# One 512-column matmul for the high and low inputs of the residual projections, and two broadcasts issued later

## The chip, the cores and the metric

The kernel runs on one core of one Trainium2 chip. The metric is the device time of one execution in microseconds (us), taken as the median of several. TensorE's engines are called PE (matmuls) and PEld (weight loads), VectorE DVE, ScalarE ACT, GpSimd POOL, and SyncE SP.

## The reference

A two-layer block of attention mixers, an indexer, layer norms, a neighbourhood attention, a Fourier mixer, a convolution mixer, cross attention to a memory and convolutional feed-forward nets, on 256 tokens of width 1024, all in float32. What this study is about are the products that are added to the residual stream. There are eight of them, and the first two feed a layer norm:

```
x = layer_norm(ALPHA * x + y @ w_out, ...)     # twice: phases oa, ob
h = h + concat([yf, ya]) @ w_out               # oab
h = h + (gate_b * conv) @ w_out                # oc
h = h + attention(rms(h), memory) @ wo         # ox0, ox1
h = h + (gelu(g) * u) @ w_down                 # fd0, fd1
```

Everything is kept near float32 accuracy by splitting each operand of a projection into a high part (rounded to the matmul's input format) and a low part (what is left), and by adding three products: high x high, high x low, low x high.

## The kernel before

The activations stand as channels x tokens: `h` is the residual stream (128 partitions, 8 tiles of channels, 256 tokens), `xh` and `xl` are the high and low part of the normalised stream, `yh` and `yl` those of a mixer's output.

The weights come from memory in 153 chunks of 1 MB, through four slots `raw` that SP refills. A chunk covers 256 output channels and 1024 input channels, in two halves (`j` = 0, 1) of 128 output channels. For each half ACT writes the high part of the weights, `hi` (L904, `wh`), and DVE the low part, `lo` (L1354, `wl`). PE counts the halves that it has used in `w_used`, and `hi(h)` waits until half h-4 has been used, since `wh` and `wl` hold two chunks.

`project` (L402 and on) multiplies a chunk: for each half 8 tiles `k` of 128 input channels, and for each of these 16 weight tiles three matmuls of 128x128 weights by 256 tokens (L428). A phase is a run of chunks with one operand; its name is that of its weights. With `ready` a phase starts on an operand that is still being made: its first chunk (its first two, where an output takes two chunks) is in the "early" order, which does the tiles 0 to 5 of both halves first, waits for each tile's high part before the first two products and for its low part before the third, and then does tiles 6 and 7. Phases without hooks run their four chunks as two rounds of a loop over the same code, so the early order comes back at every other chunk. `project_tokens` (L499) is for phases whose outputs stand as tokens x channels; its matmuls have 512 columns.

`hooks` are small pieces of work put between the matmuls of a phase, keyed by chunk, half and tile. A norm needs two of them on PE. `stats` (L542) adds the squares (for a layer norm first the values) over the channels; it waits for the sums `acc` that POOL makes (L1846). Then DVE scales them (L1439), POOL takes the power -1/2 (L1863), DVE puts it on a diagonal (L1434), and `bcast` (L549) spreads it over the partitions into bank 5, from where ACT copies it (L988).

In a residual phase each engine does the following for each output (256 channels, one chunk; two chunks in fd0 and fd1, "deep"):

- DVE (`residual`): `x_low` of the output before (L1427), two `lo`, then it waits for PE, and adds the output in PSUM to `h` (L1458; L1461 in oa and ob, where `h` is scaled by ALPHA as well).
- ACT (`residual`): one `hi`, the square of the output before for POOL's sum (L950), one more `hi`, then it waits for DVE's addition and writes `xh` of it (`x_high`, L958). In oa and ob ACT has only the `hi`.
- POOL: it sums the four squares into `acc` (L1846).

The outputs lie in PSUM banks 0 to 3: a phase has a pair (0 and 1, or 2 and 3), an output takes one bank (its two halves side by side), and consecutive phases alternate between the pairs. `enter` waits until the phase before the last, which had the same pair, has been read.

Of the kernel before, what the change touches and what calls it, by code (L numbers as in the profile page):

```python
# [19 lines left out]
F32 = mybir.dt.float32  # L20
# [4 lines left out]
P = 128  # L25
# [49 lines left out]
def schedule():  # L75
# [3 lines left out]
    def add(name, chunks, reader, outs=None, deep=1, wide=False):  # L79
# [7 lines left out]
        p.wide = wide  # L87
# [12 lines left out]
    add("oa", 4, "dve")  # L100
# [6 lines left out]
    add("ob", 4, "dve")  # L107
# [7 lines left out]
    add("oab", 4, "dve")  # L115
    for l in "01":
# [5 lines left out]
        if l == "1":  # L122
            add("oc", 4, "dve")
        add("qx" + l, 4, "dve")
        add("attX" + l, 0, "dve", 4)
        add("ox" + l, 4, "dve")
        add("fu" + l, 8, "dve")
        add("fg" + l, 8, "dve")
        add("fd" + l, 8, "dve", deep=2)
# [46 lines left out]
def build(nc, w, xt, memt, vecs, cst, wkw, dft, rpb, out):  # L176
    ctx = ExitStack()
    with ctx:
# [11 lines left out]
        xh = sb("xh", [P, KT, S], F32R)  # L190
        xl = sb("xl", [P, KT, S], F32R)
        yh = sb("yh", [P, 2 * KT, S], F32R)
        yl = sb("yl", [P, 2 * KT, S], F32R)
# [21 lines left out]
        bank = [ctx.enter_context(nc.psum_tensor(f"bank{i}", [P, 512], F32)) for i in range(8)]  # L215
# [180 lines left out]
        def _(pe):  # L396
            def enter(p):

                if p.before is not None:
                    pe.wait_ge(evac[p.before.reader], p.before.end)  # L400

            def project(name, oh, ol, ready=None, hooks={}, tile0=0):  # L402
# [4 lines left out]
                p = PH[name]  # L407
                enter(p)
                per = 2 * p.deep

                def round_(i, first, hooks=hooks):
                    for c in range(per):
                        n = per * i + (p.n0 + c)
                        slot = (p.n0 + c) % 2
                        b = b3(p.pair + c // p.deep)
                        k0 = (c % p.deep) * KT
# [5 lines left out]
                        def product(k, q, j):  # L422
# [12 lines left out]
                        def steps(j, tiles):  # L435
# [269 lines left out]
            def then(*calls):  # L705
                def f():
                    for call, *args in calls:
# [16 lines left out]
            project("ga", xh, xl, hooks={(1, 0, 2): then((turn_unit, 8)), (1, 1, 3): then((turn_unit, 9)),  # L724
                                         (2, 1, 3): lambda: stats("mem"), (3, 1, 4): lambda: bcast("mem")})
# [129 lines left out]
            for l in "01":  # L855
# [8 lines left out]
                if l == "1":  # L864
                    project("oc", yh, yl, y_ready("conv", g_lo, GBASE["conv"], 2))
# [1196 lines left out]
```

## Time and profile before

| | |
|---|---|
| median of 3 runs | 1037.66 us (1037.25 to 1040.43) |
| the profiled execution | 1037.87 us, span 1036.1 us |
| busy: PE, PEld | 1011.9 us (98%), 945.6 us (91%) |
| busy: DVE, ACT, POOL | 664.6 us (64%), 530.3 us (51%), 165.8 us (16%) |
| mean granted TensorE clock | 0.995 of full speed |
| DMA | 172.56 MB, mean 167 GB/s |

The span is the time from the first to the last instruction of the profiled execution. A busy share is that of the whole span; matmuls overlap their successors in the rows, so the time from one start to the next is what a matmul takes from PE, and its own duration is longer. "Idle" in a row is the time in which the engine stood still just before the instruction, and the name behind it is what it waited for.

### The profile page before, as it was taken

The numbers are of one execution on the slowest core, as the hardware profiler recorded it, in microseconds if no ns is written. First come the engines' busy times: TensorE is split into PE (matmuls) and PEld (weight loads), VectorE is DVE, ScalarE is ACT, GpSimd is POOL, SyncE is SP. The second block draws the span as 40 slices with busy tenths as digits, with TensorE's granted clock in tenths as the row PEclk, the third lists the DMA queues.
The fourth block names the chain that finished last, engine by engine and source line by source line (L and its number), as shares of the span: only waits on it lengthen the run. The fifth ranks groups of instructions, "written<-read, shape, count | busy, mean of one in ns | idle before, by whom it ended". The sixth has DMA issues, their size and how long they took to land.

```text
span 1036.1 us, 18469 instructions
## 1 busy us (share of the span) xinstructions
PE 1011.9 (98%) x7450; PEld 945.6 (91%) x7450; DVE 664.6 (64%) x1022; ACT 530.3 (51%) x804; POOL 165.8 (16%) x146
## 2 busy tenths in 40 slices
PE   9999899999999999999999999999999999999996
PEld 7779669999978998888999999999998999999996
DVE  4779675754457678566456569755576655658852
ACT  4547473454477455455345447544354545436641
POOL 0001022300026231001002005210034200103500
PEclk9999999999999999999999999999999999999998
DMA  9634415465440536425514554447546433455431
GB/s 357 228 122 163 160 45 203 163 221 185 168 157 2 200 141 228 179 88 204 197 45 162 200 203 162 163 176 270 203 163 237 151 141 122 166 200 175 150 122 40
DMA packets 24971, 172.56 MB, mean 167 GB/s; under 512 B 2768, under 2 KB 2896, under 8 KB 4432
## 3 DMA queue, kind: packets, MB, share of 16 engines
q1 hardware_dynamic: 23328, 160.86, 43.4%
q10 hardware_dynamic: 1584, 10.88, 2.7%
q8 instruction: 40, 0.66, 0.2%
q14 instruction: 19, 0.16, 0.0%
HBM read 166.49 MB, written 5.24 MB: 166 GB/s over the span
## 4 chain that ended last, share of the span: by engine, by line
PE 79%; DVE 9%; ACT 5%; issue 3%; DMA 1%; POOL 1%; SPq 1%; POOLq 0%; DVEq 0%; ACTq 0%
PE bank L428 54%; PE bank L499 14%; DVE wl L1354 3%; ACT wh L904 2%; DVE work L1731 2%; PE bank L624 2%; PE bank L578 1%; DMA raw<-w 1%; PE bank L606 1%; POOL acc L1846 1%; DVE work L1734 1%; PE bank L626 1%; PE bank L542 1%; ACT work L1271 1%; PE bank L701 1%
## 5 line engine op out<-in xcount | busy, mean ns | idle before, releaser
L1354 DVE TENSOR_TENSOR wl<-raw,wh 128x1024 fp32r<-128x1024 f32 x300 | 385.1, 1291 | 241.0 <-ACT wh L904 239.9
L904 ACT ACTIVATE wh<-raw 128x1024 fp32r<-128x1024 f32 x300 | 311.9, 1054 | 284.9 <-PE bank L428 221.9
L428 PE MATMUL bank<-xh,wh 128*128 128x256 f32 x1152 | 320.1, 285 | 0.0
L428 PE MATMUL bank<-xh,wl 128*128 128x256 f32 x1152 | 318.0, 283 | 0.0
L428 PE MATMUL bank<-xl,wh 128*128 128x256 f32 x1152 | 295.7, 284 | 0.0
L428 PEld LDWEIGHTS bank<-xh,wl 128*128 128x128 f32 x1152 | 221.3, 192 | 0.3
L428 PEld LDWEIGHTS bank<-xh,wh 128*128 128x128 f32 x1152 | 221.1, 192 | 0.3
L428 PE MATMUL bank<-yh,wh 128*128 128x256 f32 x768 | 209.0, 285 | 0.8 <-ACT yh L1275 0.8
L428 PEld LDWEIGHTS bank<-xl,wh 128*128 128x128 f32 x1152 | 207.8, 192 | 0.1
L428 PE MATMUL bank<-yh,wl 128*128 128x256 f32 x768 | 207.0, 283 | 0.0
L428 PE MATMUL bank<-yl,wh 128*128 128x256 f32 x768 | 178.4, 283 | 1.4 <-DVE yl L1749 1.4
L428 PEld LDWEIGHTS bank<-yh,wh 128*128 128x128 f32 x768 | 147.3, 192 | 1.9 <-ACT yh L1275 1.2
L428 PEld LDWEIGHTS bank<-yh,wl 128*128 128x128 f32 x768 | 147.3, 192 | 0.2
L428 PEld LDWEIGHTS bank<-yl,wh 128*128 128x128 f32 x768 | 130.1, 192 | 1.8 <-DVE yl L1749 1.8
L499 PE MATMUL bank<-wh,xh 128*128 128x512 f32 x176 | 69.1, 414 | 1.7 <-ACT wh L904 1.4
L499 PE MATMUL bank<-wl,xh 128*128 128x512 f32 x176 | 65.5, 394 | 0.0
L499 PE MATMUL bank<-wh,xl 128*128 128x512 f32 x176 | 65.2, 393 | 0.0
L1846 POOL TENSOR_TENSOR acc<-work 128x512 f32<-128x512 f32 x10 | 16.3, 1633 | 270.1 <-ACT work L950 270.1
L1879 POOL TENSOR_TENSOR work<-work,qz 128x512 f32<-128x512 f32 x18 | 29.3, 1625 | 137.5 <-ACT work L1271 136.2
L499 PEld LDWEIGHTS bank<-wh,xh 128*128 128x128 f32 x176 | 32.9, 190 | 12.4 <-issue 6.2
L958 ACT ACTIVATE xh<-h,vec 128x256 fp32r<-128x256 f32 x48 | 21.8, 502 | 42.2 <-DVE h L1458 42.1
L1846 POOL TENSOR_TENSOR acc<-acc,work 128x512 f32<-128x512 f32 x19 | 30.6, 1608 | 77.8 <-ACT work L950 77.6
(173 smaller groups left out, 1120.2 us busy)
## 6 DMA issues: line engine op xcount, KB each, us to landing
raw<-w SPq DMA_DIRECT2D x149, 1024.0 KB, 4.8
k_scratch<-kt ACTq DMA_DIRECT2D x2, 1024.0 KB, 8.6
kt<-k_scratch ACTq DMA_DIRECT2D x2, 1024.0 KB, 6.1
h<-xt SPq DMA_DIRECT2D x4, 256.0 KB, 5.8
raw<-w SPq DMA_DIRECT2D x2, 512.0 KB, 5.6
cs<-cst SPq DMA_DIRECT2D x1, 1024.0 KB, 12.4
v<-memt ACTq DMA_DIRECT2D x1, 1024.0 KB, 7.5
m_scratch<-yh ACTq DMA_DIRECT2D x1, 1024.0 KB, 3.9
```

Source lines behind the costliest of these rows:

```text
L428: return pe.matmul(b[:, j, :], weights, o_[:, kk, :], start=k0 + k == 0 and q == 0 and (j == 0 or not both_open), stop=k0 + k == KT * p.de ...
L499: mm = pe.matmul(bank[p.pair + t][:, :], (oh, oh, ol)[q][:, tile0 + k, t * P:t * P + P], (wh, wl, wh)[q][:, slot, half, e * 2 * CW:(e + 1) ...
L542: mm = pe.matmul(bank[4][:, t:t + 1], part[:, t * P:t * P + P], ones[:, 0:1], start=(e == 0), stop=(e == len(parts) - 1))
L578: mm = pe.matmul(bank[4 + a % 2][:, rows(name)[t]], l, r, start=(j == 0), stop=(j == len(ops) - 1))
L606: mm = pe.transpose(bank[6 + a % 2][:, at:at + P], pr[:, key:key + P], ident)
L624: pe.matmul(o, v[:, 0, sl], wk(4 + a % 2)[:, 0:S], start=True, stop=False)
L904: act.activation(wh[:, n % 2, j, :], raw[:, n % RAW_SLOTS, j, :], ACT.Copy).then_inc(hi_ready, 1)
L958: ins = act.activation(xh[:, m, :], h[:, m, :], ACT.Copy, scale=vc(gain, m))
L1354: dve.tensor_tensor(wl[:, n % 2, j, :], raw[:, n % RAW_SLOTS, j, :], wh[:, n % 2, j, :].bitcast(F32), ALU.subtract).then_inc(lo_ready, 1)
L1731: both(*[dve.scalar_tensor_tensor(cv[:, j, :], cp[:, j, 0:S], vc(taps, 2 * c + j), cv[:, j, :], ALU.mult, ALU.add) for j in range(2)])
L1846: pool.tensor_tensor(acc[:, :, :], a, source(c), ALU.add).then_inc(acc_done, 1)
L1879: pool.tensor_tensor(wk3(7 + c % 2), a, b, ALU.mult).then_inc(pf_ready, 1)
```

## The change

The low and the high part of an operand become two planes of one tensor (`xx`, `yy`), and the eight PSUM banks one tensor. Nothing is computed otherwise by that alone. The eight residual phases get `apart`:

```diff
-        p.pair = 2 * (len(order) % 2)
+        p.wide, p.apart = wide, apart
+        p.prev = order[-1] if order else None
         p.before = order[-2] if len(order) >= 2 else None
+        p.pair = 0 if p.prev is None else p.prev.pair if p.prev.apart else 2 - p.prev.pair
...
-    add("oa", 4, "dve")
+    add("oa", 4, "dve", apart=True)
...
-        xh = sb("xh", [P, KT, S], F32R)
-        xl = sb("xl", [P, KT, S], F32R)
+        xx = sb("xx", [P, 2, KT, S], F32R)
+        xh, xl = [xx[:, q, :, :] for q in range(2)]
...
             def enter(p):
-                if p.before is not None:
+                if p.prev is not None and p.prev.apart:
+                    pe.wait_ge(evac[p.prev.reader], p.prev.end - 1)
+                elif p.before is not None:
                     pe.wait_ge(evac[p.before.reader], p.before.end)
...
                         b = b3(p.pair + c // p.deep)
+                        if p.apart:
+                            b = banks[:, p.pair ^ 2 * (c // p.deep):, :]
+                            if c == p.deep:
+                                pe.wait_ge(evac[p.prev.reader], p.prev.end)
...
+                            if p.apart:
+                                at = slice(S, 2 * S) if q == 2 else slice(0, S)
+                                return pe.matmul(b[:, j, at], weights, o_[:, kk, :], start=k0 + k == 0 and q == 0,
+                                                 stop=k0 + k == KT * p.deep - 1 and q == 2, skip_group_check=True)
...
+                        def apart_product(k, j):
+                            pe.matmul(b[:, j, :], wh[:, slot, j, k * P:k * P + P], operand[:, :, tile0 + k0 + k, :],
+                                      start=k0 + k == 0, stop=False, skip_group_check=True)
+                            return pe.matmul(b[:, j, 0:S], wl[:, slot, j, k * P:k * P + P], oh[:, tile0 + k0 + k, :],
+                                             start=False, stop=k0 + k == KT * p.deep - 1, skip_group_check=True)
...
-                                for q in range(2 if early else 0, 3):
-                                    mm = product(k, q, j)
+                                if p.apart and not early:
+                                    mm = apart_product(k, j)
+                                else:
+                                    for q in range(2 if early else 0, 3):
+                                        mm = product(k, q, j)
...
+            def apart(p, o):
+                q = p.pair ^ 2 * (o % 2)
+                return banks[:, q:q + 2, 0:S], banks[:, q:q + 2, S:2 * S]
...
-                        if alpha is None:
+                        if p.apart:
+                            main, low = apart(p, o)
+                            if alpha is None:
+                                chain(dve.tensor_tensor(hc, main, hc, ALU.add))
+                            else:
+                                chain(dve.scalar_tensor_tensor(hc, hc, alpha, main, ALU.mult, ALU.add))
+                            dve.tensor_tensor(hc, low, hc, ALU.add).then_inc(dve_evac, 1)
+                        elif alpha is None:
...
-            project("ga", xh, xl, hooks={(1, 0, 2): then((turn_unit, 8)), (1, 1, 3): then((turn_unit, 9)),
-                                         (2, 1, 3): lambda: stats("mem"), (3, 1, 4): lambda: bcast("mem")})
+            project("ga", xx, hooks={(1, 0, 2): then((turn_unit, 8)), (1, 1, 3): then((turn_unit, 9)),
+                                         (2, 1, 3): lambda: stats("mem")})
...
-                (0, 1, 1): first_scores, (1, 0, 1): second_scores, (2, 0, 1): lambda: score_pair(4, 5),
+                (0, 0, 1): lambda: bcast("mem"), (0, 1, 1): first_scores, (1, 0, 1): second_scores, (2, 0, 1): lambda: score_pair(4, 5),
...
-            project_tokens("zf", xh, xl, x_ready("mix0"), {(0, 1, 1): lambda: stats("mix0"), (1, 0, 1): lambda: bcast("mix0")})
+            project_tokens("zf", xh, xl, x_ready("mix0"), {(0, 1, 1): lambda: stats("mix0"), (1, 1, 0): lambda: bcast("mix0")})
...
-                (0, 0): lambda: spread("mem", rb_m), (1, 1): lambda: exponentials("A", 0),
+                (0, 1): lambda: spread("mem", rb_m), (1, 1): lambda: exponentials("A", 0),
```

In an `apart` phase an output takes two banks, one for each half `j`; columns 0 to 255 of a bank hold high x high plus high x low, columns 256 to 511 hold low x high. Outside the early order two matmuls take the place of three. The outputs alternate between the pairs, so the second output of a phase waits until all of the phase before has been read. DVE adds the two parts to `h` one after the other, each over both banks; `chain` makes the second addition wait for the end of the first.

The rows that follow are the order of the instructions in the built programs (engine's queue, one row for like ones in succession). First PE in phase oa, where the early chunk ends and the other one begins: the last product of the chunk, what the loop does between them, and the first weight tile. Before:

```order
L428 MATMUL bank<-yl,wh 128x256
L433 REGISTER_ALU
L428 MATMUL bank<-yh,wh 128x256
L428 MATMUL bank<-yh,wl 128x256
L428 MATMUL bank<-yl,wh 128x256
```

The same place of the changed program (`yy` is the tensor with both parts):

```order
L442 MATMUL banks<-yy,wh 128x256 x2
L432 REGISTER_ALU
L456 ISA
L450 MATMUL banks<-yy,wh 128x512
L452 MATMUL banks<-yy,wl 128x256
```

The weight tile has one matmul of 512 and one of 256 columns in place of three of 256, with two weight loads in place of three. Next DVE in phase ox0, from the first output's addition to the second's. Before:

```order
L1458 TENSOR_TENSOR h<-bank,h 128x512
L1427 SCALAR_TENSOR_TENSOR xl<-h,vec,xh 128x256 x2
L1354 TENSOR_TENSOR wl<-raw,wh 128x1024 x2
L1458 TENSOR_TENSOR h<-bank,h 128x512
L1427 SCALAR_TENSOR_TENSOR xl<-h,vec,xh 128x256 x2
```

The same place of the changed program:

```order
L1491 TENSOR_TENSOR h<-banks,h 128x512
L1494 TENSOR_TENSOR h<-banks,h 128x512
L1453 SCALAR_TENSOR_TENSOR xx<-h,vec,xx 128x256 x2
L1380 TENSOR_TENSOR wl<-raw,wh 128x1024 x2
L1491 TENSOR_TENSOR h<-banks,h 128x512
L1494 TENSOR_TENSOR h<-banks,h 128x512
```

Each output has one more addition on DVE, 32 in all, ahead of everything that follows it. Last PE around the memory's broadcast. Before, it stands near the end of phase ga, with 9 matmuls of ga behind it:

```order
L428 MATMUL bank<-xl,wh 128x256
L549 MATMUL bank<-diag,ones 128x256
L428 MATMUL bank<-xh,wh 128x256
L428 MATMUL bank<-xh,wl 128x256
L428 MATMUL bank<-xl,wh 128x256
```

In the changed program it stands in phase va, behind the 12 matmuls of va's first half chunk:

```order
L525 MATMUL banks<-wh,xx 128x512 x2
L525 MATMUL banks<-wl,xx 128x512
L525 MATMUL banks<-wh,xx 128x512
L575 MATMUL banks<-diag,ones 128x256
L525 MATMUL banks<-wh,xx 128x512
L525 MATMUL banks<-wl,xx 128x512
```

It has moved past 21 matmuls: 9 of 256 columns and 12 of 512. The one of `mix0` moves past the 12 matmuls of the last half chunk of zf that followed it.

## Rows read from the trace of the kernel before

**Rows 1.** The page's part 1: busy us and share of the span.

```profile
PE 1011.9 (98%) x7450; PEld 945.6 (91%) x7450; DVE 664.6 (64%) x1022; ACT 530.3 (51%) x804; POOL 165.8 (16%) x146
```

**Rows 2.** The chain that ended last: start, us, engine, line, instructions.

```profile
476.21 21.79 PE bank L499 x96
...
538.40 28.78 PE bank L428 x240
```

**Rows 3.** PE's timeline around the memory's broadcast: start, us, instruction, idle before.

```profile
103.25 0.28 PE L428 MATMUL bank<-xl,wh 128*128 128x256 f32 x1
106.22 0.70 PE L549 MATMUL bank<-diag,ones 128*128 128x256 f32 x2 [2.69 <-DVE diag L1434]
...
110.75 0.39 PE L499 MATMUL bank<-wh,xh 128*128 128x512 f32 x1
```

**Rows 4.** PE in stretches: stretch, length, busy, PEclk (granted clock), DMA.

```profile
106.00:108.00 2.00, 1.78 (x10) 0.77 0.74 311
108.00:110.00 2.00, 2.00 (x7) 0.50 0.03 8
110.00:112.00 2.00, 2.00 (x9) 0.87 0.00 0
```

**Rows 5.** PE's timeline at the broadcast of mix0.

```profile
398.53 0.70 PE L549 MATMUL bank<-diag,ones 128*128 128x256 f32 x2 [0.99 <-DVE diag L1434]
```

**Rows 6.** DVE's timeline in phase ox0.

```profile
545.76 0.68 DVE L1458 TENSOR_TENSOR h<-bank,h 128x512 f32<-128x512 f32 x1
...
550.98 0.68 DVE L1458 TENSOR_TENSOR h<-bank,h 128x512 f32<-128x512 f32 x1
...
556.14 1.23 DVE L1354 TENSOR_TENSOR wl<-raw,wh 128x1024 fp32r<-128x1024 f32 x1 [1.32 <-ACT wh L904]
557.28 0.68 DVE L1458 TENSOR_TENSOR h<-bank,h 128x512 f32<-128x512 f32 x1
...
561.36 1.99 DVE L1354 TENSOR_TENSOR wl<-raw,wh 128x1024 fp32r<-128x1024 f32 x1 [0.25 <-ACT wh L904]
563.27 0.68 DVE L1458 TENSOR_TENSOR h<-bank,h 128x512 f32<-128x512 f32 x1
```

**Rows 7.** ACT's timeline in phase ox0, between the same additions.

```profile
546.48 0.91 ACT L958 ACTIVATE xh<-h,vec 128x256 fp32r<-128x256 f32 x2 [1.90 <-DVE h L1458]
547.29 1.04 ACT L904 ACTIVATE wh<-raw 128x1024 fp32r<-128x1024 f32 x1
548.24 0.62 ACT L950 ACTIVATE work<-h 128x512 f32<-128x512 f32 x1
548.76 1.04 ACT L904 ACTIVATE wh<-raw 128x1024 fp32r<-128x1024 f32 x1
...
555.04 1.06 ACT L904 ACTIVATE wh<-raw 128x1024 fp32r<-128x1024 f32 x1 [0.96 <-PE bank L428]
```

**Rows 8.** POOL's timeline in phase ox0 and behind it.

```profile
554.22 1.75 POOL L1846 TENSOR_TENSOR acc<-work 128x512 f32<-128x512 f32 x1 [15.56 <-ACT work L950]
560.52 1.74 POOL L1846 TENSOR_TENSOR acc<-acc,work 128x512 f32<-128x512 f32 x1 [4.54 <-ACT work L950]
565.55 1.42 POOL L1846 TENSOR_TENSOR acc<-acc,work 128x512 f32<-128x512 f32 x1 [3.29 <-ACT work L950]
```

**Rows 9.** PE's timeline in phase fu0, tile 6 of the early chunk and the norm's sums.

```profile
565.58 0.28 PE L428 MATMUL bank<-xh,wh 128*128 128x256 f32 x1
...
567.03 1.05 PE L542 MATMUL bank<-ones,acc 128*128 128x1 f32 x8
```

**Rows 10.** POOL's timeline at the end of phase oa.

```profile
184.34 1.29 POOL L1846 TENSOR_TENSOR acc<-acc,h 128x512 f32<-128x512 f32 x1 [2.05 <-DVE h L1461]
```

**Rows 11.** DVE's timeline at the end of phase oa, the low part behind the last addition.

```profile
184.60 2.11 DVE L1354 TENSOR_TENSOR wl<-raw,wh 128x1024 fp32r<-128x1024 f32 x1 [0.40 <-ACT wh L904]
```

**Rows 12.** DVE's timeline behind phase oab: the low parts for vx0.

```profile
481.18 3.93 DVE L1354 TENSOR_TENSOR wl<-raw,wh 128x1024 fp32r<-128x1024 f32 x3 [0.59 <-ACT wh L904]
```

**Rows 13.** DVE's timeline at the end of fd1.

```profile
1024.03 0.69 DVE L1458 TENSOR_TENSOR h<-bank,h 128x512 f32<-128x512 f32 x1 [6.91 <-PE bank L428]
```

More of the change, by code:

```diff
@@ L77, in schedule, with add @@
     order = []
-    def add(name, chunks, reader, outs=None, deep=1, wide=False):
+    def add(name, chunks, reader, outs=None, deep=1, wide=False, apart=False):
         nonlocal at
@@ L106, in schedule @@
     add("attB", 0, "dve", 8)
-    add("ob", 4, "dve")
+    add("ob", 4, "dve", apart=True)
     add("kx1", 4, "dve")
@@ L114, in schedule @@
     add("attN", 0, "dve", 4)
-    add("oab", 4, "dve")
+    add("oab", 4, "dve", apart=True)
     for l in "01":
@@ L189, in build @@
         h = sb("h", [P, KT, S])
-        xh = sb("xh", [P, KT, S], F32R)
-        xl = sb("xl", [P, KT, S], F32R)
-        yh = sb("yh", [P, 2 * KT, S], F32R)
-        yl = sb("yl", [P, 2 * KT, S], F32R)
+        xx = sb("xx", [P, 2, KT, S], F32R)
+        yy = sb("yy", [P, 2, 2 * KT, S], F32R)
+        xh, xl = [xx[:, q, :, :] for q in range(2)]
+        yh, yl = [yy[:, q, :, :] for q in range(2)]
         qz = sb("qz", [P, NH, S])
@@ L214, in build @@
         erec = sb("erec", [P, 28, 2])
-        bank = [ctx.enter_context(nc.psum_tensor(f"bank{i}", [P, 512], F32)) for i in range(8)]
+        banks = ctx.enter_context(nc.psum_tensor("banks", [P, 8, 512], F32))
+        bank = [banks[:, i, :] for i in range(8)]
         k_scratch = nc.dram_tensor("k_scratch", [2, P, KT * S], F32, kind="Internal").ap()
@@ L397, in enter, with project @@
             def enter(p):
-                if p.before is not None:
+                if p.prev is not None and p.prev.apart:
+                    pe.wait_ge(evac[p.prev.reader], p.prev.end - 1)
+                elif p.before is not None:
                     pe.wait_ge(evac[p.before.reader], p.before.end)
-            def project(name, oh, ol, ready=None, hooks={}, tile0=0):
+            def project(name, operand, ready=None, hooks={}, tile0=0):
                 p = PH[name]
+                oh, ol = [operand[:, q, :, :] for q in range(2)]
                 enter(p)
@@ L743, in _ @@
                            2, PH["attA"], "va")
[L744 removed]
+            project("oa", yy, y_ready("A", g_lo, GBASE["A"], 1))
             pe.wait_ge(m_lo, 4)
[L747 to L750 removed]
+            project("kx0", yy, tile0=KT, hooks=layer_norm_hooks("0"))
+            project("gb", xx, x_ready("B"))
+            project("qb", xx)
+            project("kb", xx)
             tri = c_("tri")
@@ L1370, in chunks @@
                         dve.wait_ge(w_used, 2 * n + 2)
-                        evacuate(c // p.deep, b3(p.pair + c // p.deep % 2))
+                        evacuate(c // p.deep, apart(p, c) if p.apart else b3(p.pair + c // p.deep % 2))
                     if between is not None:
@@ L1690, in f @@
                         dve.wait_ge(rb_ready, RBS[name] + 1)
-                    dve.tensor_tensor(dst[:, 2 * c:2 * c + 2, :], b, rb[:, :].unsqueeze(1).broadcast_to([P, 2, S]),
-                                      ALU.mult).then_inc(dve_evac, 1)
+                    d = dst[:, 2 * c:2 * c + 2, :]
+                    if isinstance(b, tuple):
+                        chain(dve.tensor_tensor(d, *b, ALU.add))
+                        b = d
+                    dve.tensor_tensor(d, b, rb[:, :].unsqueeze(1).broadcast_to([P, 2, S]), ALU.mult).then_inc(dve_evac, 1)
                 return f
```

40 lines of the change are left out of this document (17 added, 23 removed).

## The prediction, made before the changed kernel had run

> **What bounds the kernel now.** I read the page's busy shares first: PE is busy for 98% of the span [rows 1]. So nearly everything that PE saves is saved, and a wait that PE gets is lost, unless something else limits the stage. The chain of waits gives the price of a matmul: 240 matmuls of 256 columns in 28.78 us, 119.9 ns each, and 96 of 512 columns in 21.79 us, 227.0 ns each [rows 2]. The durations in the rows (280 and 390 ns) overlap and are no price. A chunk without waits is 48 x 119.9 ns = 5.76 us.
>
> Then I looked for PE's own waits. The two broadcasts that move are two of the largest: 2.69 us for the memory's [rows 3], 0.99 us for mix0's [rows 5]. The first costs more than its wait, since behind it the granted clock falls to 0.50 of full speed (the 1.2 GHz level) and is back at 2.4 GHz only within the stretch from 110 to 112 us [rows 4].
>
> Last I read the three other engines in a residual phase, because their queues get the new additions [rows 6, 7, 8].
>
> **The matmuls.** A weight tile costs 3 x 119.9 = 359.7 ns now, and 227.0 + 119.9 = 346.9 ns with one matmul of each kind: 12.8 ns less. Six phases have two chunks outside the early order, two have four: 20 chunks x 16 tiles = 320 tiles, 4.1 us, 0.21 us for a chunk. This is small because the columns stay the same; only one start of three goes. The operand of 512 columns now comes in two runs of 256, for which no row exists. Bounds: nothing saved if the two runs cost what the start saves; and at most 113 ns a tile (the 119.9 of the matmul that goes, if the wider one cost only some 7 ns more), which the 227.0 ns excludes. I take 4.1 us and keep 0 and 4.1.
> The Trainium skill (TensorE: Matmul & The Clock Gate, Back-to-back issue gap) gives N/2.4 + 2.5 ns for a start; by it the tile would save 2.5 ns and all tiles 0.8 us. The rows show some 13 ns over the columns' time, so the rows decide.
>
> **The broadcasts.** Memory: from 103.25 us to 110.75 us PE issues 10 matmuls of 256 columns (1.20 us) and 6 of 512 (1.36 us) beside the broadcast; without wait and at full clock that takes 2.56 us, and it took 7.50 us [rows 3]. The broadcast itself, re-inserted later, costs about 0.35 us (its start to the next matmul's, 106.22 to 106.57 in the timeline of which rows 3 are a part). Gain 4.6 us; I take 4.5. The diagonal is ready at 106.2 us. PE would be through ga at 104.5 and through va's first half chunk (12 x 0.227) at 107.2, so the broadcast no longer waits. ACT's copy `spread` is moved by one step too, behind a `hi` that waits for that same half chunk, and the first scores that wait for it come another 12 matmuls later. This frees time that nothing after it needs.
> mix0: PE ends zf about 2.7 us after the old place, the wait was 0.99 us; gain 1.0 us. The bound of both from below is their waits alone, 3.7 us together, from above 5.9 us.
>
> **The second addition.** One costs 0.68 us, and it can't start before the first ended: 0.71 us for each output [rows 6]. PE doesn't wait for it directly. But ACT's `x_high` does, and a loop goes through it: addition, `x_high`, `hi`, square, `hi`, `lo`, next addition. It takes 545.76 to 550.98, 5.22 us [rows 6, 7], against a chunk of 5.76. With 0.71 it takes 5.93 us, and the chunk now only 5.55. So the loop becomes longer than the work that hid it. Step by step through ox0:
> - The first addition starts where it did (it waits for PE), and ends 0.71 later; the second output is done 1.42 later.
> - ACT waited 0.96 us for PE at 555.04 [rows 7], so it has its third `hi` only 0.36 later. But the square is 1.42 later, and with it POOL's first sum: from 554.22 to 555.64. Now it meets DVE's two `lo`. In the rows, a `lo` that begins while POOL runs takes 1.99 in place of 1.23 us (561.36, POOL from 560.52), and a sum that begins during a `lo` takes 1.75 us in place of 1.42 or less [rows 6, 8, 10]: the one waits for the other. So the `lo` of 556.14 is held until POOL ends near 557.4, its follower starts at 558.4 and not 557.28: 1.13 later, done 1.84 later.
> - The fourth output: all is 1.84 later, plus 0.71: done 2.55 later.
> The norm's sum behind it ends at 565.55 + 1.42 = 566.97, and PE takes it at 567.03 without having waited [rows 8, 9]: no slack. So PE's `stats` comes 2.5 us later in absolute time, whatever PE saved before. Seen from PE: it reaches tile 6 of fu0 at 565.16, waits 2.3 us for `xh`, 0.45 for `xl`, 0.2 for the sum. ox1 and oc have the same queues and the same loop: three times 2.5 us later where 0.42 us earlier was to be had, 8.8 us in all. Without the meeting with POOL the lateness is 1.8 us each, the lower bound: 6.7 us.
> That rule stands in the Trainium skill too (SBUF - State Buffer, Who interferes with whom): a DVE instruction with two SBUF inputs contends with GpSimd's reads, one with a single SBUF input does not. By it the additions themselves, which read PSUM, are not held, and the `lo` are, as above.
>
> The other phases. oab is followed by vx0, which needs no `x`; but the third `lo` behind it (481.18) [rows 12] comes 2.55 later, done at 485.0, and PE wants it after 36 matmuls of vx0 (475.8 + 8.2 = 484.0) [rows 2]: 1.0 us. oa and ob: ACT isn't in the loop, yet DVE's last addition is pushed by POOL's third sum; it ends at 185.3 in place of 184.2, and then DVE's `lo`, which had to wait for ACT and let POOL go first (184.60 behind 184.34) [rows 10, 11], is ready at once and goes first. The sum ends near 187.7, PE wants it at 186.6: 1.1 us each, from 0 if POOL gets in first. fd0: an output takes 11.5 us against a loop of 6, so only 0.71 us remains and the slack at the norm is about 2 us: nothing. fd1 ends the kernel: its last addition waited 6.91 us for PE [rows 13], all behind it is in a row: 0.7 us.
>
> **The sum.** -4.1 - 4.5 - 1.0 + 8.8 + 1.0 + 2.2 + 0.7 = +3.1 us. On the profiled execution's 1037.87 us this is 1041.0; the median of the runs shown is 0.2 us lower, so 1040.8 us.
>
> **Rivals.**
> - *The lateness stays hidden.* If the fourth output were in time (the loop cut somewhere, or slack that I don't see), only -9.6 + 0.7 is left: 1029. Against it stands the sum that PE takes 0.06 us after its end. With half of the lateness 1033 or so. Chance 0.20, and this is the case on the other side; it decides where the lateness of a residual phase falls under 1 us.
> - *The meeting with POOL falls out the other way.* The lateness is 1.8 us three times, oa, ob and oab cost 0.35 together: -9.6 + 6.7 + 0.35 + 0.7 = -1.9 us, 1035.8. The two stretched rows speak against it, the changed times of all engines for it. Chance 0.20.
> - *The clock falls at the new waits.* PE would wait 2.3 us and then 0.45 and 0.2 within 2 us more, three times; after 2.69 us it fell, after 0.99 it didn't [rows 3, 4, 5]. Each fall costs some 3.6 us at half speed, 1.8 us: 1042.6 to 1046.2. Chance 0.22.
> - *The forecast*, 1041 with 2 us on either side: 0.38.
>
> **How the numbers follow.** Runs of this kernel can tell about 0.3%, 3.1 us, from no change: 1034.6 to 1040.8. Faster: the first rival nearly whole, a little of the second, 0.22. Same: most of the second and half of the forecast, 0.36. Slower: the other half and the clock, 0.42. The forecast alone is 1039 to 1043. The range for all, 1033 to 1045, leaves out the first rival's full gain and three falls of the clock.
>
> **What would show it.** The matmuls of the non-early chunks: pairs of 347 ns from start to start; 360 would mean that nothing is saved. No wait at the memory's broadcast, and a granted clock of 1.00 from 104 to 114 us. DVE's additions in ox0: the last ends 2.5 us later relative to the phase's start. PE's waits: in fu0, fu1 and qx1 for ACT's `xh` (about 2.3 us each) and the sum; in vx0 for `wl`; in kx0 and kx1 for POOL. If the waits for `xh` are under 1 us, the step on the loop is wrong, and the time is under 1035. If the clock's mean is under 0.995, the new waits cost more than their length.

## The result, and the profile after

| | before | changed |
|---|---|---|
| median of the runs | 1037.45 us (4 runs, 1036.99 to 1040.43) | 1051.5 us (4 runs, 1051.11 to 1054.87) |
| profiled execution, span | 1037.87, 1036.1 us | 1051.63, 1049.8 us |
| mean granted TensorE clock | 0.995 | 0.986 |

The changed kernel is slower: the ratio is 1.0135, with a 95% interval of 1.0117 to 1.0154. The forecast was 1040.8 us with a range from 1033 to 1045, so the time lies outside it. The page's first part of the changed kernel:

```profile
PE 1019.2 (97%) x7130; PEld 937.3 (89%) x7130; DVE 684.2 (65%) x1054; ACT 529.7 (50%) x804; POOL 169.3 (16%) x146
```

PE issues 320 matmuls fewer than in [rows 1] and is yet busy for 7 us more. A busy time that rises with less work points to a slower clock, and the clock's mean says the same. (Both means also hold a fall at the kernel's end, 9.4 us before and 11.2 us in the changed kernel.) PE's waits, longest first in total (total, times, longest):

```profile
PE banks L444 <- ACT xx L984: 6.3, 3, 2.1
...
PE banks L568 <- ACT work L976: 2.3, 1, 2.3
PE banks L525 <- DVE wl L1380: 1.9, 2, 1.4
```

The first row is new. It is PE's wait for `xh` of tile 6 in the first chunk of a phase behind a norm, three times. The second is the wait of the last norm, the third contains the one in vx0. Here is one of the three waits for `xh`, in fu0, from PE's timeline (start, us, instruction, idle before):

```profile
564.87 0.39 PE L444 MATMUL banks<-xx,wh 128*128 128x256 f32 x1 [2.08 <-ACT xx L984]
...
565.79 0.71 PE L444 MATMUL banks<-xx,wh 128*128 128x256 f32 x3 [0.17 <-DVE xx L1453]
...
567.37 1.70 PE L568 MATMUL banks<-ones,acc 128*128 128x1 f32 x8
...
572.91 0.65 PE L575 MATMUL banks<-diag,ones 128*128 128x256 f32 x2
```

And PE in stretches over the same time (stretch, length, busy of PE, PEld, DVE, ACT and POOL, granted clock, DMA):

```profile
564.00:566.00 2.00, 0.95 (x5) 0.74 (x6) 0.88 (x2) 2.00 (x4) 0.52 (x1) 1.00 0.31 131
566.00:568.00 2.00, 2.00 (x12) 2.00 (x11) 1.63 (x1) 1.35 (x2) 0.87 (x1) 0.55 0.00 0
568.00:570.00 2.00, 2.00 (x10) 2.00 (x11) 0.16 (x1) 0.00 (x0) 0.66 (x1) 0.50 0.42 70
570.00:572.00 2.00, 2.00 (x11) 2.00 (x11) 1.62 (x3) 0.00 (x0) 0.04 (x1) 0.50 1.01 418
572.00:574.00 2.00, 2.00 (x14) 1.95 (x13) 0.00 (x0) 0.40 (x2) 0.00 (x0) 0.75 0.11 45
```

The eight matmuls of the norm's sum (567.37) take 1.70 us, where they took 1.05 in [rows 9], and the stretches say why: behind the wait the clock is granted at 0.50 (the 1.2 GHz level). The time at the lower level is 1.8 + 2 + 2 + 1.0 = 6.8 us, by the share that each clock figure lacks. By the same reckoning [rows 4] gives 0.9 + 2 + 0.5 = 3.4 us. That was the only fall in the trace of the kernel before, apart from the one at its end. The falls behind oc and ox1 last as long; this is the one in qx1 (behind oc):

```profile
828.00:830.00 2.00, 1.82 (x11) 1.62 (x12) 1.41 (x3) 1.82 (x3) 1.39 (x1) 0.75 0.00 0
830.00:832.00 2.00, 2.00 (x12) 2.00 (x11) 0.91 (x1) 0.48 (x1) 0.00 (x0) 0.50 0.00 0
832.00:834.00 2.00, 2.00 (x10) 2.00 (x11) 1.04 (x4) 0.00 (x0) 0.70 (x1) 0.50 0.90 283
834.00:836.00 2.00, 2.00 (x12) 2.00 (x11) 0.73 (x1) 0.00 (x0) 0.00 (x0) 0.54 0.57 242
```

DVE in ox0, the rows that answer to [rows 6]:

```profile
543.09 0.68 DVE L1491 TENSOR_TENSOR h<-banks,h 128x512 f32<-128x512 f32 x1
543.81 0.69 DVE L1494 TENSOR_TENSOR h<-banks,h 128x512 f32<-128x512 f32 x1
...
549.04 0.69 DVE L1491 TENSOR_TENSOR h<-banks,h 128x512 f32<-128x512 f32 x1
...
553.85 1.99 DVE L1380 TENSOR_TENSOR wl<-raw,wh 128x1024 fp32r<-128x1024 f32 x1 [0.25 <-ACT wh L930]
555.76 0.68 DVE L1491 TENSOR_TENSOR h<-banks,h 128x512 f32<-128x512 f32 x1
...
562.48 0.68 DVE L1491 TENSOR_TENSOR h<-banks,h 128x512 f32<-128x512 f32 x1
563.19 0.69 DVE L1494 TENSOR_TENSOR h<-banks,h 128x512 f32<-128x512 f32 x1
```

From the first addition's start to the last one's end it takes 563.88 - 543.09 = 20.8 us, against 563.95 - 545.76 = 18.2 before: 2.6 us, forecast 2.55. The loop takes 5.95 us (forecast 5.93), and the `lo` of 553.85 is stretched to 1.99 us, because POOL has been at it since 553.01:

```profile
553.01 1.75 POOL L1887 TENSOR_TENSOR acc<-work 128x512 f32<-128x512 f32 x1 [17.01 <-ACT work L976]
```

### The profile page after: what moved, and what is told of

It is laid out like the page before. It is cut to its first block, busy times and chain, and to the rows that moved or that the text cites. A ratio compares the mean times of both kernels' runs of the same rounds, so it can differ in the third digit from the quotient of the medians.

```text
span 1049.8 us, 17861 instructions
## 1 busy us (share of the span) xinstructions
PE 1019.2 (97%) x7130; PEld 937.3 (89%) x7130; DVE 684.2 (65%) x1054; ACT 529.7 (50%) x804; POOL 169.3 (16%) x146
## 4 chain that ended last, share of the span: by engine, by line
PE 69%; DVE 12%; ACT 10%; issue 4%; POOL 3%; DMA 1%; SPq 1%; POOLq 0%; DVEq 0%; ACTq 0%
PE banks L444 34%; PE banks L525 12%; PE banks L442 6%; DVE wl L1380 5%; ACT wh L930 5%; PE banks L450 3%; DVE work L1772 2%; POOL acc L1887 2%; PE banks L650 1%; PE banks L452 1%; DVE h L1494 1%; PE banks L604 1%; DMA raw<-w 1%; PE banks L632 1%; PE banks L568 1%
## 5 line engine op out<-in xcount | busy, mean ns | idle before, releaser
L444 PE MATMUL banks<-xx,wh 128*128 128x256 f32 x2304 | 429.0, 287 | 6.7 <-ACT xx L984 6.3
L444 PEld LDWEIGHTS banks<-xx,wh 128*128 128x128 f32 x2304 | 366.7, 194 | 8.6 <-ACT xx L984 6.9
L444 PE MATMUL banks<-xx,wl 128*128 128x256 f32 x1152 | 320.8, 286 | 0.0
L444 PEld LDWEIGHTS banks<-xx,wl 128*128 128x128 f32 x1152 | 224.1, 194 | 0.3
L442 PE MATMUL banks<-yy,wh 128*128 128x256 f32 x640 | 119.1, 285 | 2.3 <-DVE yy L1790 1.4
L525 PE MATMUL banks<-wh,xx 128*128 128x512 f32 x352 | 114.8, 402 | 1.1 <-ACT wh L930 0.8
L450 PE MATMUL banks<-yy,wh 128*128 128x512 f32 x320 | 113.2, 397 | 0.0
L442 PEld LDWEIGHTS banks<-yy,wh 128*128 128x128 f32 x640 | 100.4, 191 | 3.9 <-DVE yy L1790 1.8
L452 PE MATMUL banks<-yy,wl 128*128 128x256 f32 x320 | 89.8, 281 | 0.0
L442 PE MATMUL banks<-yy,wl 128*128 128x256 f32 x320 | 80.2, 283 | 0.0
L450 PEld LDWEIGHTS banks<-yy,wh 128*128 128x128 f32 x320 | 60.1, 188 | 13.8
L442 PEld LDWEIGHTS banks<-yy,wl 128*128 128x128 f32 x320 | 61.0, 191 | 0.1
L452 PEld LDWEIGHTS banks<-yy,wl 128*128 128x128 f32 x320 | 60.5, 189 | 0.0
L1887 POOL TENSOR_TENSOR acc<-work 128x512 f32<-128x512 f32 x10 | 16.3, 1631 | 273.5 <-ACT work L976 273.5
L444 PE MATMUL banks<-yy,wh 128*128 128x256 f32 x256 | 48.7, 287 | 0.0
```

The source lines that it names most:

```text
L442: return pe.matmul(b[:, j, at], weights, o_[:, kk, :], start=k0 + k == 0 and q == 0, stop=k0 + k == KT * p.deep - 1 and q == 2, skip_group ...
L444: return pe.matmul(b[:, j, :], weights, o_[:, kk, :], start=k0 + k == 0 and q == 0 and (j == 0 or not both_open), stop=k0 + k == KT * p.de ...
L450: pe.matmul(b[:, j, :], wh[:, slot, j, k * P:k * P + P], operand[:, :, tile0 + k0 + k, :], start=k0 + k == 0, stop=False, skip_group_check ...
L452: return pe.matmul(b[:, j, 0:S], wl[:, slot, j, k * P:k * P + P], oh[:, tile0 + k0 + k, :], start=False, stop=k0 + k == KT * p.deep - 1, s ...
L525: mm = pe.matmul(bank[p.pair + t][:, :], (oh, oh, ol)[q][:, tile0 + k, t * P:t * P + P], (wh, wl, wh)[q][:, slot, half, e * 2 * CW:(e + 1) ...
L1887: pool.tensor_tensor(acc[:, :, :], a, source(c), ALU.add).then_inc(acc_done, 1)
```

## Where the 14 us went

PE's norm instructions are the same in number and order in both programs, so their starts can be compared one by one. The times are those of the two timelines.

| PE's instruction | before | changed | later by | step | what lies between |
|---|---|---|---|---|---|
| stats of the memory | 96.37 | 96.41 | 0.04 | | |
| stats behind oa | 186.91 | 183.21 | -3.70 | -3.7 | the memory's broadcast, oa |
| stats behind ob | 365.20 | 362.31 | -2.89 | +0.8 | ob |
| stats behind oab | 503.59 | 500.92 | -2.67 | +0.2 | mix0's broadcast, oab, vx0 |
| broadcast in fu0 | 570.19 | 572.91 | +2.72 | +5.4 | ox0 and its norm |
| broadcast behind fd0 | 711.37 | 713.73 | +2.36 | -0.4 | fd0 |
| broadcast in qx1 | 827.93 | 835.92 | +7.99 | +5.6 | oc and its norm |
| broadcast in fu1 | 891.47 | 904.70 | +13.23 | +5.2 | ox1 and its norm |
| the last broadcast | 1028.99 | 1042.78 | +13.79 | +0.6 | fd1 |

Three steps (5.4, 5.6 and 5.2) hold 16.3 us, more than the whole loss of 13.8; all the others together gain 2.5. Two causes can be told apart in the three: the late norm and the clock behind it.

## The experiments

The comparisons below are with the kernel before on the same chip: 1038.1 us for the first four, 1037.7 us for the next four, 1037.8 us for the last. It had 1037.45 us beside the changed kernel's 1051.5, so a difference between runs of two groups is good to some 0.7 us. What a single phase costs is read from the traces, between the same norm instructions as in the table.

**Only the broadcasts.** The kernel before with the hooks of `mem` and `mix0`, and ACT's `spread`, moved as in the change.

> The kernel before with only the two broadcasts moved. Theory A (the broadcasts gain what was forecast, the residual phases lose everything): 1037.5 - 4.6 - 1.0 = 1032 us, no fall of the clock near 107 us, mean clock above 0.995. Rival B (the broadcasts' gain is given back to later waits, so part of the 14 us is theirs): 1035 or more.

1033.1 us (1032.2 to 1034.0), ratio 0.9952, interval 0.9935 to 0.9968. By the same instructions as in the table, the memory's move brings 4.5 us (between its stats and those behind oa) and mix0's 1.3 us. So the rest of the change costs 1051.5 - 1033.1 = 18.4 us.

**The second addition alone.** All matmuls are those of before.

```diff
-                            dve.tensor_tensor(hc, b, hc, ALU.add).then_inc(dve_evac, 1)
...
+                            chain(dve.scalar_tensor_tensor(hf, bf, 0.5, hf, ALU.mult, ALU.add))
+                            dve.scalar_tensor_tensor(hf, bf, 0.5, hf, ALU.mult, ALU.add).then_inc(dve_evac, 1)
```

> The kernel before with the two broadcasts moved and all matmuls as before (three of 256 columns, one bank for an output), but DVE adds each output in two chained steps: half of the bank, then the other half again (in oa and ob the second step adds zero times the bank). It isolates the second addition. Theory A (the second addition alone makes the norm late, and the clock falls at the waits): the steps of the three norms in the changed kernel, 5.4 + 5.6 + 5.2, and 1.5 at vx0, 1.3 in oa and ob, 0.7 at the end come on top of 1032: 1051 to 1052 us, with three falls of the granted clock of some 6.8 us each. Rival B (the wider matmul, its operand in two runs or the two banks do it): 1032 to 1034, clock above 0.995. Rival C (lateness without the clock): 1042.

1051.25 us, from 1047.82 (mean clock 0.992) to 1053.93 (0.985), 18.2 us above the broadcasts alone. One more instruction of 0.7 us in DVE's queue is enough for this harm; neither the wider matmul nor the two banks are needed for it. PE's longest wait is of the same kind as in the changed kernel, 1.8 us in place of 2.1 at most:

```profile
PE bank L428 <- ACT xh L958: 5.4, 3, 1.8
```

In its profiled execution the fall in fu0 is shorter than the two that follow (6.8 us each), 0.8 + 2 + 0.6 = 3.4 us by its stretches:

```profile
564.00:566.00 2.00, 0.96 (x5) 0.87 (x5) 0.93 (x3) 1.92 (x4) 0.35 (x1) 0.80 0.34 143
566.00:568.00 2.00, 2.00 (x11) 2.00 (x10) 1.51 (x1) 1.52 (x2) 1.04 (x1) 0.50 0.00 0
568.00:570.00 2.00, 2.00 (x17) 2.00 (x16) 0.28 (x2) 0.00 (x0) 0.57 (x1) 0.85 0.27 53
```

From the stats to the broadcast in fu0 it takes 0.25 us longer than in the kernel before; in the changed kernel it takes 2.4 us longer.

**The wider matmuls alone.** The changed kernel without the line of the second addition (it computes the product low x high and leaves it out of the output).

> The changed kernel without the second addition: the product low x high is computed but never added to the output, all else is left. Theory A: 1032 less the matmuls' 4.1: 1028 us, no fall of the clock before the end, no wait of PE in fu0, fu1 and qx1 above 0.5 us. Rival B (the matmul form or the reading of two banks costs): above 1032.

1030.31 us, ratio 0.9931 (0.9914 to 0.9947). The waits for `xh` and the falls behind them are gone, as Theory A has it, but the gain over the broadcasts alone is 2.8 us in the medians and 2.1 in the traces (from the memory's stats to the last), where 4.1 was expected. Two things are in this. First the pairs: this is where the wide matmuls of oa's two chunks begin and end in the changed kernel (each chunk has 16 pairs; the last row of a group is the first matmul behind it).

```profile
161.60 0.40 PE L450 MATMUL banks<-yy,wh 128*128 128x512 f32 x1
...
167.25 0.28 PE L442 MATMUL banks<-yy,wh 128*128 128x256 f32 x1
...
173.02 0.40 PE L450 MATMUL banks<-yy,wh 128*128 128x512 f32 x1
...
178.57 0.28 PE L444 MATMUL banks<-yy,wh 128*128 128x256 f32 x1
```

5.65 us or 353 ns a pair in the first chunk, 5.55 us or 347 ns in the second. All six phases of four chunks have this pattern, and in fd0 and fd1 all pairs before the end take 353 ns. 14 chunks x 16 x 6.4 ns + 6 chunks x 16 x 12.4 ns = 2.6 us. Second, behind ox0, oc and ox1 0.2 to 0.3 us of it is waited away at each norm, since the norm isn't earlier.

**Work in place of the wait.** 17 matmuls of 256 columns more, written to a bank that nothing reads, ahead of the wait for tile 6 in fu0, qx1 and fu1.

```diff
                                 for k in tiles:
+                                    if first and j == 0 and k == KT - 2:
+                                        for _ in range(fill):
+                                            pe.matmul(bank[7][:, 0:S], wh[:, slot, 0, 0:P], oh[:, 0, :],
+                                                      start=True, stop=True, skip_group_check=True)
...
```

> The changed kernel with 17 more matmuls of 256 columns (2.0 us, into a bank that nothing reads) ahead of the wait for tile 6 in the first chunk of fu0, qx1 and fu1, so that PE works where it waited. Theory A (the clock falls because PE stands still there): no fall in these three phases, each gets back 3.0 to 3.4 us: 1041 to 1042 us, though PE does 51 matmuls more. Rival B (the clock falls for another reason, or at the remaining waits of 0.2 to 0.5 us as well): 1050 to 1052.

1045.64 us (1043.87 to 1046.35): 5.9 us faster than the changed kernel, with 51 matmuls more. In fu0 PE reaches the same place without a wait, and the clock stays:

```profile
565.36 2.20 PE L464 MATMUL banks<-xx,wh 128*128 128x256 f32 x17
...
568.53 0.62 PE L444 MATMUL banks<-xx,wh 128*128 128x256 f32 x3 [0.17 <-DVE xx L1457]
```

```profile
566.00:568.00 2.00, 1.94 (x17) 1.74 (x16) 1.02 (x2) 1.34 (x4) 0.00 (x0) 1.00 0.71 295
568.00:570.00 2.00, 1.83 (x15) 1.48 (x13) 1.41 (x3) 1.90 (x3) 1.40 (x1) 1.00 0.00 0
```

By PE's broadcasts the three norms get back 2.8, 3.0 and 2.7 us: 8.5 us is what the falls behind them cost, and 16.3 - 8.5 = 7.8 is the lateness. The expected 1041 to 1042 was missed by 4 us: each norm got back some 2.8 us where 3.0 to 3.4 were expected, and the larger part is something that I hadn't counted on. Behind oa and ob, where PE has run the same instructions as in the changed kernel and waits the same 0.88 us (first the changed kernel's row, then this one's), the clock now fell, for 1.4 + 2.0 = 3.4 us by the stretches:

```profile
183.21 0.61 PE L568 MATMUL banks<-ones,acc 128*128 128x1 f32 x4 [0.88 <-POOL acc L1887]
```

```profile
183.15 1.05 PE L572 MATMUL banks<-ones,acc 128*128 128x1 f32 x8 [0.88 <-POOL acc L1891]
```

```profile
184.00:186.00 2.00, 2.00 (x13) 2.00 (x14) 1.72 (x4) 0.00 (x0) 0.00 (x0) 0.65 0.99 414
186.00:188.00 2.00, 2.00 (x9) 1.82 (x9) 0.05 (x1) 0.00 (x0) 0.00 (x0) 0.50 0.10 41
```

Behind ob it is the same. By the norm instructions the two falls cost 2.8 us.

**A shorter loop.** On ACT the square goes behind the second `hi` of a chunk, in all residual phases; all else is the changed kernel.

```diff
-                        if j == 1 and c % p.deep == 0 and o >= 1:
-                            square(stat, o - 1, h[:, 2 * o - 2:2 * o, :])
                         if 2 * c + j >= split:
                             hi(2 * n + 3 + j)
+                        if j == 1 and c % p.deep == 0 and o >= 1:
+                            square(stat, o - 1, h[:, 2 * o - 2:2 * o, :])
```

> The changed kernel; only on ACT, in the residual phases, the square of the output before stands behind the second high part and no longer ahead of it. DVE's second low part then starts about 0.5 us earlier and POOL's sum about 0.6 later, behind both low parts, so the loop through the two additions takes 5.8 us in place of 5.95 to 6.7. Theory A (the loop makes the norm late, the wait makes the clock fall): the last output of ox0, ox1 and oc is 2.0 us earlier, PE's wait for its high part falls from 2.1 to 0.5 us or less, no fall of the clock there: 1051.5 - 8.6 (the falls, as the filled waits showed) - 6.0 = 1037 us, 1035.5 to 1039. Rival B (POOL's later sum becomes the last link, the norm stays late): 1042 to 1050.

1036.17 us (1034.98 to 1040.31). No instruction is left out, and 15 us are gone, 8.5 of them the falls of the clock by what the filled waits showed. DVE's two `lo` now stand back to back, and additions start 5.6 to 5.8 us apart:

```profile
544.87 0.68 DVE L1491 TENSOR_TENSOR h<-banks,h 128x512 f32<-128x512 f32 x1
...
548.21 2.36 DVE L1380 TENSOR_TENSOR wl<-raw,wh 128x1024 fp32r<-128x1024 f32 x2
550.48 0.68 DVE L1491 TENSOR_TENSOR h<-banks,h 128x512 f32<-128x512 f32 x1
...
562.61 0.69 DVE L1494 TENSOR_TENSOR h<-banks,h 128x512 f32<-128x512 f32 x1
```

The last one ends 563.3 - 544.87 = 18.4 us behind the first, 2.4 less than in the changed kernel. PE's longest wait at tile 6 of fu0 is 0.17 us, and the clock doesn't fall at any of the three norms. POOL's second sum begins during a `lo` and is the one that is stretched, to 1.94 us, where it holds up nothing:

```profile
561.20 1.94 POOL L1887 TENSOR_TENSOR acc<-acc,work 128x512 f32<-128x512 f32 x1 [3.68 <-ACT work L976]
```

The clock did fall behind oa and ob in the profiled execution. Of the ten runs, six with a clock of 0.993 to 0.995 took 1035.0 to 1036.7, and the three with 0.991 took 1037.9 to 1040.3; the tenth had 0.992 and 1036.7. So the same program has these falls in some executions and not in others.

**Second additions only where they are needed.** Chunks in the early order have three matmuls a tile anyway. Their outputs (0 and 2) stay in one bank with one addition.

```diff
-                        if p.apart:
-                            b = banks[:, p.pair ^ 2 * (c // p.deep):, :]
+                        if p.apart and c >= p.deep:
+                            b = banks[:, p.pair ^ 2:, :]
...
-                        if p.apart:
+                        if p.apart and o % 2:
                             main, low = apart(p, o)
```

> The changed kernel, but the outputs made in early chunks, which have three matmuls a tile anyway, stay in one bank with one addition: 16 second additions in place of 32, all wider matmuls kept. The last output of ox0, ox1 and oc is 1.2 us earlier than in the changed kernel by the loop's times, PE's wait for its high part about 0.9 us. Theory A with no fall of the clock at that wait: 1051.5 - 8.6 - 3.6 = 1039 us; with falls at all three: 1047. Rival B (lateness does not go by the number of additions): 1050 or more.

1036.60 us (1035.53 to 1037.63). This is 2.4 us better than expected, because oa, ob and vx0 are hardly late any more either. By the norm instructions oa costs 0.2 us and ob 0.1 beyond the broadcasts' kernel, where the changed kernel costs 0.8 each, and vx0 nothing, where the changed kernel costs 1.4. PE waits 0.2 us for POOL's last sum in oa, in place of 0.88. At the norms behind ox0, oc and ox1 PE still waits for `xh`, but in the profiled execution the clock stays up, and the mean of all ten runs (0.994 to 0.996) leaves no room for three falls of 6.8 us:

```profile
560.87 0.38 PE L440 MATMUL banks<-xx,wh 128*128 128x256 f32 x1 [0.67 <-ACT xx L980]
561.79 0.62 PE L440 MATMUL banks<-xx,wh 128*128 128x256 f32 x3 [0.18 <-DVE xx L1449]
```

```profile
562.00:564.00 2.00, 2.00 (x17) 1.85 (x17) 1.64 (x1) 1.35 (x2) 0.89 (x1) 1.00 0.00 0
```

**Both edits.** Second additions only at odd outputs, and ACT's square behind the second `hi`.

> Both of the two edits before: second additions only at odd outputs, and ACT's square behind the second high part. Theory A: the last output of ox0, ox1 and oc comes at 18.3 us of the phase's first addition in place of 20.8, and PE waits 0.4 us or less: 1051.5 - 8.6 - 7.5 = 1035.4 us, perhaps 0.5 less at vx0. It should lie below the first two, above the kernel with only the broadcasts (1033.1), since oa and ob stay late by 1.0 us each.

1031.73 us (1031.27 to 1033.22), ratio 0.9943 (0.9921 to 0.9964). It is 3.7 us better than expected, again mostly since oa, ob and vx0 are free. PE has no wait for `xh` left, and each of the three norms is 0.4 us earlier than in the broadcasts' kernel, so the wider matmuls' gain arrives.

**Additions by halves.** As the one before, and the two additions of an odd output are made for half `j` = 0 while PE works on half 1.

```diff
                     for j in range(2):
+                        if j == 1 and o % 2 and c % p.deep == p.deep - 1:
+                            add_half(0)
                         if 2 * c + j >= split:
                             lo(2 * n + 3 + j)
```

> As the one before, and the two additions of an odd output are made by halves: those of the first bank already while PE works on the second half of the chunk, so that behind the chunk stand two additions of 256 columns (some 0.4 us each) in place of two of 512. Theory A (only what stands behind the chunk's end counts): nothing of the second addition is left on the path, oa, ob and vx0 get back their 1.0 to 1.5 us too: the kernel without the second addition took 1030.3, so 1030 to 1031.5 us. Rival B (four more waits and additions in DVE's queue hold up its low parts): 1034 or more.

1033.89 us (1032.51 to 1034.14), 2.2 us worse than the kernel that it starts from. The gain of Theory A didn't come; what came is the cause that Rival B names, at nearly its price. By PE's norm instructions, oa and ob gain 0.25 us each over that kernel, but the three norms behind ox0, oc and ox1 come 1.0 us later. DVE in ox0 shows why:

```profile
550.70 0.68 DVE L1499 TENSOR_TENSOR h<-banks,h 128x512 f32<-128x512 f32 x1
...
554.46 0.42 DVE L1483 TENSOR_TENSOR h<-banks,h 128x256 f32<-128x256 f32 x1
...
555.25 2.01 DVE L1376 TENSOR_TENSOR wl<-raw,wh 128x1024 fp32r<-128x1024 f32 x1
557.18 0.41 DVE L1483 TENSOR_TENSOR h<-banks,h 128x256 f32<-128x256 f32 x1
```

DVE's time before PE's end is not free: the additions of the first half hold up the second `lo` by 0.8 us, into POOL's sum, and it takes 2.01 us. From the third output's addition to the fourth's it is 6.5 us, where the kernel with both edits has 552.36 to 557.25, 4.9 us.

**Five phases.** The changed kernel with ox0, ox1 and oc as before.

```diff
-            add("oc", 4, "dve", apart=True)
+            add("oc", 4, "dve")
...
-        add("ox" + l, 4, "dve", apart=True)
+        add("ox" + l, 4, "dve")
```

> The changed kernel with the wider matmuls and the second addition only in oa, ob, oab, fd0 and fd1; ox0, ox1 and oc are as before. Theory A (what is lost is lost phase by phase, 16.3 of it behind these three): 1051.5 - 16.3 + 0.9 (the three phases save nothing any more, and PE is later at their norm by nothing) = 1035 to 1036.5 us, one fall or two of 3.4 us behind oa and ob being possible (1.7 each). Rival B (the losses move to another phase): 1040 or more.

1036.90 us (1035.93 to 1039.11). The loss of these three phases doesn't move elsewhere: the steps at their norms are 0.0 us against the broadcasts' kernel. The other five together still lose 4.3 us against it in the medians (that kernel, run on the same chip, has 1032.6, see below): by the same instructions 1.9 at oa with a fall of the clock behind it, 0.8 at ob, 1.4 at vx0, 1.0 at the end; fd0 alone gains, 0.4.

**The broadcasts again**, beside the next two:

> The kernel with only the two broadcasts moved once more, to stand beside the next two on one chip. 1032.2 to 1034.0 us as in its first runs, 0.5% below the kernel before.

1032.58 us (1032.22 to 1035.04), ratio 0.9959 (0.9946 to 0.9972).

**Each where it pays.** Second additions only at odd outputs, the square last, and halves only in oa, ob and fd1.

```diff
+                    halves = alpha is not None or name == "fd1"
...
+                        if j == 1 and halves and o % 2 and c % p.deep == p.deep - 1:
+                            add_half(0)
```

> Second additions only at odd outputs, ACT's square behind the second high part, and the additions by halves only in oa, ob and fd1, where they brought 0.3, 0.3 and 0.5 us by the anchors of the two traces; in oab, ox0, ox1, oc and fd0 they stay whole, where the halves made the norm 0.55 to 0.9 us later. Theory A (each phase's loss is its own): 1031.7 - 1.1 = 1030.6 us, 1.5 to 3 us below the kernel with only the broadcasts beside it. Rival B (nothing left to win, all within noise of that kernel): 1032 to 1033.

1030.84 us (1029.91 to 1032.25), ratio 0.9943 (0.9930 to 0.9955). Of the kernels that add all three products it is the fastest, 6.9 us below the kernel before and 1.7 us below the broadcasts alone on the same chip. That 1.7 us is small beside the spread of the runs (the two ranges touch at 1032.2), but the traces agree: from the memory's stats to the broadcast in fu1 it takes 787.3 us, against 789.4 with the broadcasts alone. Its page:

```profile
PE 1008.1 (98%) x7130; PEld 928.3 (90%) x7130; DVE 670.8 (65%) x1050; ACT 530.3 (52%) x804; POOL 171.1 (17%) x146
```

With as many matmuls as the changed kernel, 7130, PE is busy for 11 us less.

**The loop written out.** The kernel with both edits, and PE's code for the residual phases unrolled (`if hooks or p.apart or p.base < 2`).

> Second additions only at odd outputs and the square behind the second high part, and PE's code of the residual phases is written out round by round in place of a loop. It asks why a pair of matmuls took 353 ns in the first round of a loop and in fd0 and fd1, and 347 ns in the second round of the short phases. Theory A (code that PE runs for the first time comes slower, and the loop's second round has it at hand): all pairs 353 ns, time up by 0.6 us to 1032.3. Rival B (it goes by the place of the chunk in its phase, by operands or by what the other engines do): 353 and 347 stay where they are, time unchanged within 0.3.

1032.31 us (1031.23 to 1033.88). The pairs stay as they were, 353 ns in the first chunk of oa and 347 in the second:

```profile
161.38 0.40 PE L446 MATMUL banks<-yy,wh 128*128 128x512 f32 x1
...
167.03 0.28 PE L440 MATMUL banks<-yy,wh 128*128 128x256 f32 x1
...
172.80 0.40 PE L446 MATMUL banks<-yy,wh 128*128 128x512 f32 x1
...
178.35 0.28 PE L440 MATMUL banks<-yy,wh 128*128 128x256 f32 x1
```

So the loop isn't the reason. Why the first chunk's pairs take 6 ns more stays open; it holds 1.4 us of the forecast's 4.1.

## Why the prediction was wrong

| term | forecast | measured | from |
|---|---|---|---|
| matmuls | -4.1 | -2.6 | the pairs, 353 and 347 ns |
| memory's broadcast | -4.5 | -4.5 | the kernel with the broadcasts alone |
| mix0's broadcast | -1.0 | -1.3 | the same |
| norms of ox0, oc, ox1, without the clock | +8.8 | +8.7 | steps 16.3, less the falls 8.5, plus the 0.3 that each phase's pairs save |
| vx0 | +1.0 | +1.7 | the step there against the broadcasts' kernel, plus 0.3 |
| oa and ob | +2.2 | +2.3 | the same |
| the end | +0.7 | +0.8 | PE's wait there for ACT, 2.3 in place of 1.5 |
| the clock behind the three norms | 0 | +8.5 | the filled waits |
| sum | +3.1 | +13.6 | the profiled executions differ by 13.8 |

**The failed step** is that the sum put the clock behind the three new waits at nothing. The forecast had the case only as a rival, "The clock falls at the new waits", with a chance of 0.22 and at "some 3.6 us at half speed, 1.8 us" each. It was the case that came, at 2.8 us each and 8.5 us in all, so its price was too low as well. Two readings of the same rows led there. The forecast itself had PE wait 2.3, 0.45 and 0.2 us in each of the three phases. [Rows 3] and [rows 4] showed a fall behind 2.69 us, [rows 5] none behind 0.99; a forecast wait of 2.3 us lies by the one that fell, and should have been the likeliest case. And the duration of a fall was taken from the one instance in [rows 4], 3.4 us (the forecast read 3.6), while these last 6.8. With the 8.5 us the sum would have been 1049.3, and with the matmuls' shortfall of 1.5, 1050.8, close to the measured 1051.5. The forecast did name the sign, a mean clock under 0.995; it came out at 0.986.

**The lateness** was right, step by step. The loop addition, `x_high`, `hi`, square, `hi`, `lo` took 5.95 us, and the meeting with POOL stretched the `lo` to 1.99 us. Counted from ox0's first addition, the next three start 0.73, 1.15 and 1.88 us later than before, where the forecast's steps give 0.71, 1.13 and 1.84. The last output was 2.6 us late and PE waited 2.08 us for it. One slip had no effect: ACT's third `hi` would be 1.42 - 0.96 = 0.46 us later, not 0.36 (it came 0.40 later). The kernel with two half additions shows that this needs nothing but DVE's extra instruction, and moving the square shows that it is this loop. The Trainium skill (SBUF - State Buffer, Who interferes with whom) gives the meeting its rule: a DVE instruction with two SBUF inputs contends with a GpSimd instruction that reads SBUF. The rows agree, since both `lo` that begin while POOL runs take 1.99 us in place of 1.23, and with the square moved, so that the sum begins during a `lo`, it is the sum that is stretched.

**The broadcasts** gained what was forecast; in the changed kernel the clock is 1.00 in all stretches from 104 to 114 us.

**The matmuls** gained 2.6 of 4.1 us. The mechanism was right, the term mis-sized: a tile saved 12.4 ns (12.8 forecast) in 6 of 20 chunks and 6.4 ns in the other 14.

**oa and ob** were late by the 1.1 us of the forecast, and neither the forecast nor its rivals had a clock fall there. It comes in some executions only.

## What to carry to other kernels

When a forecast puts a new wait on the engine that bounds the kernel, the wait's own length is only half of its price here: read which waits of the old trace had a fall of the clock behind them, and if the new one is of that length, count the fall as the likely case. Before adding an instruction to an engine that helps the bounding one, follow the loop that runs through it (addition, high part, square, low part) and compare its time with the chunk that hides it, 5.22 and then 5.95 against 5.76 us; the order of two instructions in that loop was worth 15 us, far more than the 2.6 us of matmuls that the change saved. A saving on the bounding engine reaches the end only where the work beside it has slack. At the norms behind ox0, oc and ox1 it had none, and there the matmuls' gain was waited away until the loop was shortened.

## What the hardware showed that was not expected

- Ahead of the kernel's end, every fall of the clock in these traces lasts 3.4 or 6.8 us. In the same place, fu0, it lasted 6.8 us behind a wait of 2.1 us in the changed kernel, and 3.4 us behind one of 1.8 us in the kernel with two half additions. What decides is open.
- The length of the wait alone doesn't decide whether the clock falls: behind a wait of 0.9 us in oa it fell in the profiled executions of three kernels (filled waits, square moved, five phases) and not in the changed kernel's, though PE had run the same instructions up to there. Behind the like wait in ob it fell in two of them, and not with the five phases. With second additions only at odd outputs, behind 0.67 us and 0.18 us more, it didn't fall.
- A weight tile costs 3 x 119.9 = 359.7 ns with three matmuls of 256 columns, and 347 or 353 ns with one of 512 and one of 256, by the chunk's place in its phase.
